# First expert position's tokens put into slots by one-hot products, and the gate row's broadcast issued behind the slot copies

## The reference, cut to what matters

```python
g_val, g_idx = lax.top_k(p_group, 1)                  # one group of four
e_val, e_idx = lax.top_k(p_exp, TOP_K)                # two experts in it
expert_id = g_idx * EXPERTS_PER_GROUP + e_idx
combine = jnp.sum(one_hot(expert_id, N_EXPERTS) * weight[..., None], axis=1)
hid = silu(einsum("nd,edf->nef", x, w1)) * einsum("nd,edf->nef", x, w3)
y = einsum("nef,efd->nd", hid * combine[..., None], w2)
```

## Time and profile before

| what | value |
|---|---|
| median of three runs | 986.39 us |
| span of the profiled execution, first to last instruction | 983.9 us |
| PE busy | 900.8 us (92%) |
| DVE, ACT, POOL busy | 406.7, 289.7, 263.1 us |
| mean granted TensorE clock | 0.960 of full |
| expert loop, layer 0: first up product to last down product | 390.9 to 566.9 us |
| expert loop, layer 1: the same | 794.4 to 968.5 us |

### The profile page before, as it was taken

The page is one execution under the profiler, slowest core; times in us unless marked ns, Lnnn a source line. Parts: engine busy times, 40 slices in busy tenths (PEclk is TensorE's granted clock), DMA queues, the critical chain, the costliest instruction groups (busy, mean ns, idle before and its releaser), DMA issues.

```text
span 983.9 us, 13906 instructions
## 1 busy us (share of the span) xinstructions
PE 900.8 (92%) x5729; PEld 578.3 (59%) x5729; DVE 406.7 (41%) x762; ACT 289.7 (29%) x537; POOL 263.1 (27%) x175
## 2 busy tenths in 40 slices
PE   3899999978797998998999989999999899989996
PEld 1688898755565985333333379888588743323332
DVE  1653665566635462222223463222625602222245
ACT  2632243332433243111111364121552521101112
POOL 0156353300003301233233306230360113333330
PEclk9999999998996997999999999999999889999998
DMA  9675335412424958999886543330449959999815
GB/s 379 261 257 214 129 135 204 149 44 89 171 91 145 419 177 322 403 378 401 299 313 230 186 163 129 129 130 1 174 179 417 364 187 377 403 362 380 294 64 202
DMA packets 41598, 230.08 MB, mean 234 GB/s; under 512 B 14112, under 2 KB 15168, under 8 KB 21824
## 3 DMA queue, kind: packets, MB, share of 16 engines
q1 hardware_dynamic: 22608, 189.80, 50.5%
q0 software_dynamic: 14528, 28.61, 8.1%
q10 hardware_dynamic: 4400, 10.77, 3.1%
HBM read 279.58 MB, written 19.81 MB: 304 GB/s over the span
## 4 chain that ended last, share of the span: by engine, by line
PE 75%; DVE 9%; DMA 9%; ACT 4%; issue 2%; POOL 1%; ACTq 0%; POOLq 0%; DVEq 0%
PE ps L2094 17%; PE ps L1723 8%; PE ps L2108 8%; PE ps L1725 8%; PE ps L1724 8%; PE ps L1694 4%; DMA Z<-experts_up,par 4%; PE ps L2119 2%; DMA att<-h_rows,par 2%; PE ps L1858 2%; DVE Z L1180 2%; DMA xT<-x_columns 1%; DVE Z L1059 1%; PE ps L1709 1%; PE ps L1715 1%
## 5 line engine op out<-in xcount | busy, mean ns | idle before, releaser
L547 POOL TENSOR_TENSOR wlo<-raw,whi 128x1024 fp32r<-128x1024 f32 x57 | 139.2, 2462 | 355.4 <-ACT whi L663 353.0
L2094 PE MATMUL ps<-Z,att 128*64 128x512 f32 x704 | 192.5, 605 | 6.3 <-DMA Z<-experts_up,par 6.3
L2094 PEld LDWEIGHTS ps<-Z,att 128*64 128x64 f32 x704 | 58.1, 139 | 100.6 <-issue 100.6
L1723 PE MATMUL ps<-hhi,whi 128*128 128x384 f32 x296 | 104.9, 354 | 6.7 <-DVE hlo L1295 3.0
L1724 PE MATMUL ps<-hlo,whi 128*128 128x384 f32 x296 | 101.0, 341 | 0.0
L1725 PE MATMUL ps<-hhi,wlo 128*128 128x384 f32 x296 | 100.9, 341 | 0.0
L1059 DVE TENSOR_TENSOR att<-att,ps 128x256 f32<-128x256 f32 x28 | 11.8, 421 | 190.4 <-ACT att L870 184.7
L663 ACT ACTIVATE whi<-raw 128x1024 fp32r<-128x1024 f32 x58 | 59.8, 1054 | 86.3 <-DMA raw<-weights 56.2
L2108 PE MATMUL ps<-raw,att 128*64 128x512 f32 x272 | 80.2, 598 | 0.0
L1723 PE MATMUL ps<-whi,hhi 128*128 128x256 f32 (+1 forms) x264 | 74.9, 284 | 2.4 <-DVE hlo L1570 1.7
L1724 PE MATMUL ps<-wlo,hhi 128*128 128x256 f32 (+1 forms) x264 | 73.7, 279 | 0.0
(11 more groups left out here) (332 smaller groups left out, 1487.0 us busy)
## 6 DMA issues: line engine op xcount, KB each, us to landing
raw<-weights SPq DMA_DIRECT2D x69, 1024.0 KB, 4.9
Z<-experts_up SPq DMA_DIRECT2D x26, 2048.0 KB, 10.8
raw<-experts_down SPq DMA_DIRECT2D x20, 1024.0 KB, 9.0
spare<-experts_up SPq DMA_DIRECT2D x6, 2048.0 KB, 12.1
Z<-weights SPq DMA_DIRECT2D x8, 1024.0 KB, 16.5
hf<-experts_down SPq DMA_DIRECT2D x6, 1024.0 KB, 9.1
spare<-experts_down SPq DMA_DIRECT2D x6, 1024.0 KB, 8.9
Z<-y_rows SPq DMA_DIRECT2D x12, 512.0 KB, 6.0
```

Source lines behind the costliest of these rows:

```text
L547: nc.gpsimd.tensor_tensor(unit_view(wlo, u), raw_unit(n, half), unit_view(whi, u).bitcast(F32), ALU.subtract)\
L1723: mm(out, ahi, bhi, start=start, stop=False)
L2094: last = mm(out, h[:, k, c:c + HALF], ring(BLOCK_AT[q, z])[:, k, :], start=(k == 0), stop=(k == KC - 1))
```

## The change

The rows of position 0 are no longer gathered from DRAM. DVE builds `scatter`, one 128x128 tile per token block with a one at (token, slot in position 0), from `column` and `place` (six more instructions; the tile lies on the memory of `picked[0]`). PE multiplies each of the eight chunks of `x_row` with it: 24 products of 128x128x128, into the banks in which `fill(0)` put its transposes. They stand right behind the owners' products, with the wait on the row numbers (`rows_ready`) in between since bank 7 is shared. `pick(0)` and `fill(0)` go, and so do the three `keep`s; `fill(1)` moves into the middle of `up(0)`. On ACT, `slots(0)` comes before the gate rows, `slots(1)` behind their write, and the broadcast read comes only behind `slots(1)`. In layer 0 one `ada` copy moves ahead of the `x_row` copies, the second `ada` pair goes to bank 5 and behind the products, and its last copy behind the gates' write. SP waits for `picked1` in place of `picked0`.

```diff
-PICKS = [len(range(z, POSITIONS, 3)) for z in range(3)]
+PICKS = [len(range(z, POSITIONS, 3)) - (z == 0) for z in range(3)]
...
+        scatter = picked[0][:, 0:TOK].rearrange("p (b t) -> p b t", b=NB)
...
-                    sp.wait_ge(S("picked0"), 16)
+                    sp.wait_ge(S("picked1"), 16)
...
-                for q in range(3):
-                    pick(q)
+                pick(1)
+                pick(2)
...
                 affine(2 * l + 1, l, SH2, {1: 16} if l == 0 else {})
+                if l == 0:
+                    ada_rows(17, 6)
...
-                if l == 0:
-                    ada_rows(17, 6)
-                    ada_rows(18, 6)
+                slots(0)
                 act.wait_ge(S("owners_T"), 2 * l + 2)
...
+                if l == 0:
+                    ada_rows(18, 5)
+                slots(1)
                 act.wait_ge(S("h_stored"), 16 * NB * (l + 1))
                 act.wait_ge(S("gates_out"), 32 * (l + 1))
                 act.dma_start(gate_row, ...)
-                slots(0)
-                slots(1)
                 silu(0)
...
+                dve.wait_ge(S("owners_ready"), 7 * l + 6)
+                for b in range(NB):
+                    link(V.tensor_scalar(scatter[:, b, :], column[:, b, :], place[:, b, 0:1], None, ALU.mult), back=2)
+                dve.wait_ge(S("dve_link"), count[0] - 2)
+                for b in range(NB):
+                    ins = V.scalar_tensor_tensor(out=scatter[:, b, :], in0=column[:, NB + b, :], scalar=place[:, NB + b, 0:1],
+                                                 in1=scatter[:, b, :], op0=ALU.mult, op1=ALU.add)
+                    if b < NB - 1:
+                        link(ins, back=2)
+                ins.then_inc(S("owners_ready"), 1)
...
                 if l == 0:
-                    ada(2, 6)
-                    pe.wait_ge(S("adarow_ready"), 19)
-
-                keep((0, 5)[l], bank(4, 256))
+                    pe.wait_ge(S("adarow_ready"), 18)
+                pe.wait_ge(S("owners_ready"), 7 * (l + 1))
+                for h in range(2):
+                    if h:
+                        pe.wait_ge(S("rows_ready"), 4 * l + 1)
+                    for k in range(4 * h, 4 * h + 4):
+                        for b in range(NB):
+                            last = mm(bank(6 + h, P, P * (k - 4 * h)), x_row[b][:, P * k:P * k + P], scatter[:, b, :],
+                                      start=(b == 0), stop=(b == NB - 1))
+                    last.then_inc(S("slot_T"), 1)
+                if l == 0:
+                    ada(2, 5)
...
-                keep((7, 0)[l], bank(4, 256))
-                fill(0)
-                keep((2, 4)[l], bank(4, 256))
-                fill(1)
-                up(0)
+                up(0, between=lambda: fill(1))
+                if l == 0:
+                    pe.wait_ge(S("adarow_ready"), 19)
```

More of the change, by code:

```diff
@@ L2113, in fill @@
                 def fill(q):
-                    pe.wait_ge(S(f"picked{q % 3}"), 16 * (PICKS[q % 3] * l + q // 3 + 1))
+                    pe.wait_ge(S(f"picked{q % 3}"), 16 * (PICKS[q % 3] * l + (q + 2) // 3))
                     for h in range(2):
@@ L2143, in experts @@
                 for i in range(6):
-                    pe.wait_ge(S("owners_ready"), 6 * l + i + 1)
+                    pe.wait_ge(S("owners_ready"), 7 * l + i + 1)
                     ins = mm(bank(7, POSITIONS, 64), column[:, i, :], named[:, i, :], start=(i == 0), stop=(i == 5))
```

## The result

The changed kernel takes 978.8 us (median of 7 runs, 977.9 to 982.7) against 986.4 (7 runs); the ratio is 0.9941, 95% interval 0.9924 to 0.9958, so 4 to 7.5 us faster. A second set of runs gave 0.9944 (0.9924 to 0.9963). Forecast was 977.2, range 973.7 to 982.5. The time is in the range; the gain, 5.8 us by the ratio, 6.9 by the two profiled spans (983.9 and 977.0) and 7.5 by the medians, is smaller than the 9.2 forecast, and it does not lie where the forecast put it.

What follows compares the result with a forecast made beforehand. PE, busy 900.8 of 983.9 us, was taken as the bound. Layer gains 4.7 + 4.9 = 9.6 us off the 986.4 median gave 976.8, put at 977.2 for clock variation; range 973.7 to 982.5.

Steps and rivals of the forecast that it cites:

- rival A: Layer 0's loop is a full DMA pipe, so layer 0 gains 1.2 us and layer 1 4.9: 980.3 us; chance 0.17.
- the account of layer 0: Layer 0: first up product 6.8 us earlier, 5.7 after fill(1), of which the loop keeps 4.7 us.
- up(0) at 384.2 and 788.1: First up product in layers 0 and 1, against 390.99 and 794.42 before: 6.8 and 6.3 us earlier.
- fill(1) costs what it did: Moved inside up(0) in both layers, fill(1) still takes 1.06 us, charged against the earlier start.
- The clock rival (C): PE stays at half clock through the products, both layers; nothing gained, 5.0 us slower, 991.4 us; chance 0.05.
- 4.9 us kept of 5.2: Layer 1's loop keeps 4.9 us of an entry 5.2 us earlier after fill(1); ends 2.6 and 5.2.
- The broadcast there: Layer 1: broadcast read moves 1 MB more in the loop's first 20 us; charged 0.3 us.
- pick(1) now is the first gather and lands when pick(0) did, so SP's down loads start as before: Before layer 0's loop: replacing the first gather leaves the start time of SP's down loads unchanged.
- So I let layer 0 keep 4.7 of 5.7: Layer 0's loop keeps 4.7 us of the 5.7 us gained from up(1) on; ends 1.2 and 5.7.
- Equal 19.65 and 19.39 us in the two layers: Position 6's overflow load times, layers 0 and 1; taken to show POOL's own queue, not SP's backlog, holds it.
- The signs that I had set: Position 6: load near 19.5 us, PE wait near 3; wrong if up(0) passes 388 or 792, or stalls grow over 3.

## Why the prediction was right or wrong

The time fell in the range, but the range was made to hold rival A (980.3) as well, so it does not speak for the account of layer 0. Of 4.7 and 4.9 us forecast for the two layers, about 1.6 and 4.8 came.

Right, ahead of the loops: up(0) at 384.2 and 788.1 were forecast, 384.14 and 787.10 came, the latter 7.02 us behind the owners' products where 7.3 was forecast. Products 7.09 us (6.8) and 5.46 (5.1): a row takes 0.114 us at full clock, not 0.106. The scatter tile was ready 1.5 us behind the columns (1.4). The clock was back at full from 376.7. fill(1) costs what it did. The clock rival (C) did not come: the clock rose 3.3 us into the products.

Right in layer 1: 4.9 us kept of 5.2 was forecast, 4.8 of 5.6 is the mean over the traces, and the run with a later entry shows it is the entry that brings it. The broadcast there was no burden that could be told from noise.

Wrong in layer 0, in two steps. The first is "pick(1) now is the first gather and lands when pick(0) did, so SP's down loads start as before". The gather did, the loads didn't: they also wait for the last ada product, since they go into tiles that hold ada weights, and that product had been moved behind 7.1 us of products. Before, it was done at 378.8 and hidden by the gather (380.1). The loads started 2.35 us late. Setting that right together with an entry 1.2 us earlier was worth 1.0 us, so this step is the smaller one; its own share was not separated.

The second and larger is "So I let layer 0 keep 4.7 of 5.7". It kept 1.6, near the 1.2 of rival A. Equal 19.65 and 19.39 us in the two layers were taken as proof that POOL's queue is untouched by SP's backlog. They do not show that, since position 6 asks too late to meet the backlog: in the changed kernel too its load took 19.3 us. The load of position 4, issued 31 us earlier, took 20.5 us from issue to landing against 15.5, and a gather (420.94; 426.61 before) 21.5 against 15.7. The load that PE waited for before was looked at, and not the one that it would wait for next. The rule of the Trainium skill on taking turns between queues (DMA: Bandwidth & Descriptors, Queues, rings and completion order) may hold, but it does not mean that POOL's transfers take as long whatever SP has queued, which is what I drew from it: bytes left out of SP's queue took 3.6 us of PE's waits off POOL's transfers.

Rival A came near in size (1.2 forecast, 1.6 measured) and is right that SP's transfers hold the loop, but its mechanism is not quite what came: not a full pipe that returns nothing, but a backlog on top of waits that are there anyway. The fewer bytes, the later entry and the earlier loads each end at 3.7 to 5.6 us of waits.

The signs that I had set were mixed. A was to show as a wait of 8 us at position 6; that wait fell to 1.8 us, and the 7.9 us are spread over four places. The sign that stalls in the loops must not grow by more than 3 us did speak: they grew by 3.8 us in layer 0, and layer 1's by 0.3.

The broadcast in layer 0: landing took 13.1 us, above the 11.6 of the earlier trace rows, and slot_gate waited 10.4 us for it. The rows of position 0 were done 22.6 us behind up(0)'s start against 19.8 before, 1.7 beyond fill(1)'s 1.06; I had said at most 1. It pushed POOL's next requests back by as much: the load of position 4 went out 26.45 us behind up(0)'s start. That lateness comes with the backlog: with fewer bytes or a later entry the same request went out after 24.8 us, and the kernel before has 23.7 plus 1.03 for fill(1). So of the 3.1 us wait at position 4 at most 1.6 are the late request, and the slower landing is the rest. What the broadcast's own 1 MB costs was not separated, since no run moved the broadcast alone.

## What to carry to other kernels

When a step is moved on one engine, list who waits for it on the queues as well: a load may be held by a reader of its tile that has nothing to do with it, and the wait that is written beside it in the code need not be the one that ends last. An earlier entry into a loop that streams weights is worth only as much as the pipe has room; check it by delaying the entry, which is one line, and move the loads together with the entry. To see whether one queue delays another, look at the time from issue to landing of every load that comes soon after the entry, and not only of the one that is waited for today. And here, once a gather had left the path, the wait that protected it from other traffic could go too, but not the one that protects the store ahead of the remaining gathers.

## What the runs showed of the hardware that was not expected

A store of 1.5 MB in three pieces of 0.5 MB on ACT's queue landed 10.0 to 11.5 us behind its issue when 3.1 MB of loads had been put in front of it on SP's queue some 2 us earlier, against 3.6 to 3.9 us in the changed kernel. The gather behind it could go out at 384.10 in place of 376.64. Being on another queue and smaller did not get the store through early.

The same indirect load of 2 MB, on POOL's queue, took 12.4 us with 3.1 MB less in SP's queue and 20.5 to 21.0 us with all of it.
